# Six converted weight quarters in place of four, and landed weights as three half slabs in place of two slabs, in a two-layer hybrid decoder trunk

## The reference

```python
def even_mixer(xn, ...):                     # layer 0: w_in 1024 x 8192, w_out 2048 x 1024
    aq, af, ai, bq, bk, bv, z = split(xn @ w_in)
    oa = head_rms_norm(hgrn2_chunked(aq, af, ai, lb))     # A: gated linear recurrence, 8 heads of 128
    ob = moba_attention(rotary(bq), rotary(bk), bv)       # B: causal softmax attention, 8 heads
    return (concat(oa, ob) * silu(z)) @ w_out
def odd_mixer(xn, ...):                      # layer 1: w_in 1024 x 6144, w_out 2048 x 1024
    cx, dq, dk, dv, z = split(xn @ w_in)
    oc = rglru_branch(cx, ...)                            # C: conv of width 4, gates, scan
    od = head_group_norm(retention_chunked(dq, dk, dv))   # D: retention, 8 heads
    return (concat(oc, od) * silu(z)) @ w_out
def memory_cross_attention(xn, mem, ...):    # wq 1024 x 512, wkv 1024 x 1024, wo 512 x 1024
    return softmax(q @ k.T / sqrt(128)) @ v @ wo
```

## Time and profile before

| what | value |
|---|---|
| median of 3 runs | 611.93 us |
| profiled execution | 613.36 us, span 611.6 us |
| mean granted TensorE clock | 0.993 |
| TensorE matmul, busy | 582.0 us (95%) |
| TensorE weight load, busy | 532.1 us (87%) |
| DVE, busy | 412.6 us (67%) |
| ACT, busy | 379.4 us (62%) |
| GpSimd, busy | 44.0 us (7%) |
| weights and other loads | 97.22 MB, 46.6% of the 16 DMA engines' time |
| low parts on DVE (line 936) | 176, 1266 ns each |
| high parts on ACT (line 436) | 176, 1057 ns each |
| chain that ended last | TensorE 63%, DVE 16%, ACT 9% |

### The profile page before, as it was taken

One profiled execution on the slowest core, in us unless ns is written; L12 is line 12 of the kernel. 1 busy time (PEld: TensorE's weight loads), 2 busy tenths in 40 slices (PEclk: granted clock), 3 DMA queues, 4 the chain that ended last, 5 costly groups with the idle time before them and its releaser, 6 DMA issues.

```text
span 611.6 us, 9584 instructions
## 1 busy us (share of the span) xinstructions
PE 582.0 (95%) x3850; PEld 532.1 (87%) x3850; DVE 412.6 (67%) x618; ACT 379.4 (62%) x561; POOL 44.0 (7%) x43
## 2 busy tenths in 40 slices
PE   3999998999999999999999999999989999999984
PEld 3998997999899898889988999999879998888973
DVE  3987368636966795566657773879956962776554
ACT  5864485247257765555766747679747828565752
POOL 4001003001001000100000001105010100100000
PEclk9999999999999999999999999999989999999998
DMA  7746453445444473465335455245333553356101
GB/s 228 268 141 212 140 192 124 157 138 207 139 138 143 140 268 139 140 228 183 138 138 198 147 191 192 95 141 210 138 137 138 201 213 138 122 188 240 35 1 69
DMA packets 51871, 97.82 MB, mean 160 GB/s; under 512 B 1236, under 2 KB 7668, under 8 KB 51828
## 3 DMA queue, kind: packets, MB, share of 16 engines
q1 hardware_dynamic: 51828, 97.22, 46.6%
HBM read 96.16 MB, written 1.05 MB: 159 GB/s over the span
## 4 chain that ended last, share of the span: by engine, by line
PE 63%; DVE 16%; ACT 9%; DVEq 6%; issue 3%; ACTq 2%; DMA 1%; SPq 0%
PE proj L1527 10%; PE proj L1528 10%; PE proj L1529 10%; PE proj L1545 8%; PE proj L1547 8%; PE proj L1546 8%; DVE w_lo L936 5%; PE head L1635 4%; ACT w_hi L436 3%; PE head L1724 1%; ACT xT_hi L458 1%; DVE junk L1403 1%; DVEq L1126 1%; DVE work L1125 1%; DVE xT_lo L960 1%
## 5 line engine op out<-in xcount | busy, mean ns | idle before, releaser
L936 DVE TENSOR_TENSOR w_lo<-raw_weights,w_hi 128x1024 fp32r<-128x1024 f32 x176 | 220.5, 1266 | 140.1 <-ACT w_hi L436 138.0
L436 ACT ACTIVATE w_hi<-raw_weights 128x1024 fp32r<-128x1024 f32 x176 | 184.2, 1057 | 129.4 <-PE proj L1529 74.1
L1527 PE MATMUL proj<-xT_hi,w_hi 128*128 128x256 f32 x768 | 222.0, 289 | 2.3 <-DVE xT_lo L960 1.7
L1528 PE MATMUL proj<-xT_lo,w_hi 128*128 128x256 f32 x768 | 217.2, 283 | 0.0
L1529 PE MATMUL proj<-xT_hi,w_lo 128*128 128x256 f32 x768 | 217.2, 283 | 0.0
L1527 PEld LDWEIGHTS proj<-xT_hi,w_hi 128*128 128x128 f32 x768 | 147.1, 192 | 4.6 <-issue 3.6
L1528 PEld LDWEIGHTS proj<-xT_lo,w_hi 128*128 128x128 f32 x768 | 147.2, 192 | 0.9 <-issue 0.7
L1529 PEld LDWEIGHTS proj<-xT_hi,w_lo 128*128 128x128 f32 x768 | 147.1, 192 | 0.0
L1545 PE MATMUL proj<-w_hi,y_hi 128*128 128x512 f32 x192 | 76.2, 397 | 0.0
L1547 PE MATMUL proj<-w_lo,y_hi 128*128 128x512 f32 x192 | 74.8, 390 | 0.0
L1546 PE MATMUL proj<-w_hi,y_lo 128*128 128x512 f32 x192 | 74.8, 389 | 0.0
(11 more groups left out here) (233 smaller groups left out, 687.8 us busy)
## 6 DMA issues: line engine op xcount, KB each, us to landing
raw_weights<-in_ev_w_in_dram SPq DMA_DIRECT2D x15, 2048.0 KB, 8.5
raw_weights<-in_od_w_in_dram SPq DMA_DIRECT2D x12, 2048.0 KB, 8.0
raw_weights<-in_ev_w_out_dram SPq DMA_DIRECT2D x4, 2048.0 KB, 8.0
raw_weights<-in_xa_wkv_dram SPq DMA_DIRECT2D x4, 2048.0 KB, 8.2
raw_weights<-in_od_w_out_dram SPq DMA_DIRECT2D x4, 2048.0 KB, 7.7
raw_weights<-in_xa_wq_dram SPq DMA_DIRECT2D x2, 2048.0 KB, 9.3
raw_weights<-in_xa_wo_dram SPq DMA_DIRECT2D x2, 2048.0 KB, 8.1
raw_weights<-in_ev_w_in_dram SPq DMA_DIRECT2D x4, 512.0 KB, 5.8
```

The lines of the kernel that those rows point to most:

```text
L436: act.activation(ring_quarter(w_hi, n, q), raw_quarter(n, q), ACT.Copy).then_inc(hi_ready, 1)
L936: dve.tensor_tensor(ring_quarter(w_lo, n, q), raw_quarter(n, q), ring_quarter(w_hi, n, q).bitcast(F32), ALU.subtract).then_inc(lo_ready, 1)
L1527: pe.matmul(dst, wh[:, k, :], x_hi[:, k, :], start=(k == 0), stop=False)
L1528: pe.matmul(dst, wh[:, k, :], x_lo[:, k, :], start=False, stop=False)
```

## The change

The rings hold six quarters (`RING`), quarter m in place m mod 6. The lead of a conversion over its position grows from three quarters to five: `due(p)` gives the quarters converted at position p: p + 3 up to p = 4, then two quarters at p = 5 (8, 9), one at 6 (10), two at 7 (11, 12), and p + 5 from 8 on. The landed weights are 1 MB halves of slabs ("units", u = 2n or 2n + 1) in three places (`UNITS`) with a semaphore each; SP issues unit u when unit u - 3 is converted. The wait for slab n in SP's program (line 320) stays. The constants and positions still go out at the start of the loop's pass n = 2, so behind unit 3 and its wait. `seen_f` and `prm_rows`, used at the start, are laid over `dmask`, first written in stage D.

```diff
+RING = 6
+UNITS = 3
+
+
+def due(p):
+
+    if p < 5:
+        return [p + 3]
+    return {5: [8, 9], 6: [10], 7: [11, 12]}.get(p, [p + 5])
...
-        raw = sb("raw_weights", [P, 2, 4096])
-        w_hi = sb("w_hi", [P, 4, 1024], F32R)
-        w_lo = sb("w_lo", [P, 4, 1024], F32R)
+        raw = sb("raw_weights", [P, UNITS, 2048])
+        w_hi = sb("w_hi", [P, RING, 1024], F32R)
+        w_lo = sb("w_lo", [P, RING, 1024], F32R)
...
+        seen_f = dmask[:, 0, :]
+        prm_rows = dmask[:, 1, 0:2 * P].rearrange("p (t c) -> p t c", t=2)
...
+        def dram_unit(u):
+            n, h = divmod(u, 2)
+            w = dram_slab(n)
+            if SLABS[n][2] == "F":
+                return w[:, :, 2 * P * h:2 * P * h + 2 * P]
+            if SLABS[n][2] == "T":
+                return w[:, 4 * h:4 * h + 4, :]
+            return w[:, :, 512 * h:512 * h + 512]
+
+        def unit_landings(u):
+
+            return 16 * (u // UNITS + (u % UNITS == 2))
...
-                sp.dma_start(raw[:, n % 2, :].rearrange("p (k c) -> p k c", k=4 if SLABS[n][2] == "W" else KC),
-                             dram_slab(n)).then_inc(w_landed[n % 2], 16)
+                for u in (2 * n, 2 * n + 1):
+                    if u >= UNITS:
+                        sp.wait_ge(lo_ready, 2 * (u - UNITS) + 2)
+                    sp.dma_start(raw_unit(u, SLABS[n][2]), dram_unit(u)).then_inc(w_landed[u % UNITS], 16)
...
-            def ahead(n, q):
-
-                n, q = divmod(4 * n + q + 3, 4)
+            def high_part(m):
+
+                n, q = divmod(m, 4)
                 if n >= NSLAB:
                     return
                 if n == 0:
                     act.wait_ge(first_landed[q], 16)
-                elif q == 0:
-
-                    act.wait_ge(w_landed[n % 2], 16 * ((n + 1) // 2))
-                if n >= 1:
-                    act.wait_ge(quarter_used, 4 * (n - 1) + q + 1)
+                elif q % 2 == 0:
+
+                    act.wait_ge(w_landed[(2 * n + q // 2) % UNITS], unit_landings(2 * n + q // 2))
+                if m >= RING:
+                    act.wait_ge(quarter_used, m - RING + 1)
                 act.activation(ring_quarter(w_hi, n, q), raw_quarter(n, q), ACT.Copy).then_inc(hi_ready, 1)
+
+            def ahead(n, q):
+
+                for m in due(4 * n + q):
+                    high_part(m)
```

More of the change, by code:

```diff
@@ L104, in hybrid_trunk @@
         shared = sb("shared_rows", [P, 2048])
-        prm_rows = sb("prm_rows", [P, 2, P])
         prm = sb("prm", [P, N_ROWS])
@@ L111, in hybrid_trunk @@
         causal = sb("causal", [P, 3 * P])
-        seen_f = sb("seen_f", [P, 3 * P])
         seen = sb("seen", [P, 3 * P], I32)
@@ L140, in hybrid_trunk @@
         first_landed = [sem(f"first_landed{q}") for q in range(4)]
-        w_landed = [sem(f"w_landed{i}") for i in range(2)]
+        w_landed = [sem(f"w_landed{i}") for i in range(UNITS)]
         hi_ready = sem("hi_ready")
@@ L254, in dram_slab, with raw_unit @@
             return I["xa_wo"][layer].rearrange("(k p) n -> p k n", p=P)
+        def raw_unit(u, kind):
+            return raw[:, u % UNITS, :].rearrange("p (k c) -> p k c", k=KC if kind == "F" else 4)
+        def dram_unit(u):
[8 more added lines that the diff above has]
+            return 16 * (u // UNITS + (u % UNITS == 2))
         def raw_quarter(n, q):
             kind = SLABS[n][2]
-            r = raw[:, n % 2, :]
+            r = raw_unit(2 * n + q // 2, kind)
             if kind == "F":
[L260 to L264, removed]
+                return r[:, :, P * (q % 2):P * (q % 2) + P]
+            return r[:, 2 * (q % 2):2 * (q % 2) + 2, :]
         def ring_quarter(ring, n, q):
-            return ring[:, q, :].rearrange("p (k c) -> p k c", k=KC if SLABS[n][2] == "F" else 2)
+            return ring[:, (4 * n + q) % RING, :].rearrange("p (k c) -> p k c", k=KC if SLABS[n][2] == "F" else 2)
         def bank(n, u, half=0):
@@ L929, in _, with low_part, ahead @@
         def _(dve):
-            def ahead(n, q):
-                n, q = divmod(4 * n + q + 3, 4)
+            def low_part(m):
+                n, q = divmod(m, 4)
                 if n >= NSLAB:
                     return
-                dve.wait_ge(hi_ready, 4 * n + q + 1)
+                dve.wait_ge(hi_ready, m + 1)
                 dve.tensor_tensor(ring_quarter(w_lo, n, q), raw_quarter(n, q),
                                   ring_quarter(w_hi, n, q).bitcast(F32), ALU.subtract).then_inc(lo_ready, 1)
+            def ahead(n, q):
+                for m in due(4 * n + q):
+                    low_part(m)
             def rstd(i):
```

## The result

The changed kernel took 620.05 us in the median of 7 runs (615.81 to 620.37), the kernel before, on the same chip, 613.43 us (611.83 to 615.14). The ratio of the means is 1.0094, with a 95% interval of 1.0072 to 1.0115: slower by 0.9%, 5.7 us. I had forecast slower, 616.2 us, 4.3 more than the median of three runs, in a range up to 618.1. The direction came true, the time lies outside the range.

A forecast was written before the change was run, and what follows sets the result against it. TensorE was taken as the bound, with DVE and ACT without slack in the first 50 us. Conversions 2.3, positions 0.3 and clock 1.7 summed to 4.3 us on the median of 611.93: 616.2 us, range 611.9 to 618.1.

The forecast's parts named there:

- what a longer lead can do: Conversions wait for the same quarter with either ring; at most 1.6 us of TensorE's weight waits could be removed.
- Two more conversions ahead of the scan: DVE, before line 1611: the lead made up at positions 5 and 7 delays the scan 2.3 us, bounds 1.2 to 2.6.
- The positions: SP's queue at the start: positions land behind unit 3 and delay DVE's angles by 0.3 us, bounds 0 to 1.2.
- The fit: DMA estimate, 2 us plus bytes at 436 GB/s: 1 MB lands in 4.4 us; the trace's 4.9 was preferred.
- the weight waits of slab_t: TensorE's 1.0 us of weight waits go, but later waits for DVE grow by the saving: counted nothing, bound 1.0 gained.
- the end: Last cross-attention: two conversions vanish, DVE's and ACT's waits for TensorE grow; counted nothing, bound 1.1 us gained.
- the term of the clock: Behind stage A's first wait, grown to about 3.8 us, TensorE's clock falls to half: 1.7 us, bounds 0 and 2.4.
- the base: The sum of 4.3 us was put on the median 611.93 us, not on the profiled execution's 613.36.
- the transfer rival: Rows of 1 KB and two waits per slab make halves late, 25 slabs losing 0.3 us: 623 us; chance 0.06.
- The clock holds: Rival: the same lag at the start, but no clock fall behind the stall: 614.5 us; chance 0.20.
- No change: Rival: conversions fit DVE's hole ahead of 46.58, or weight and end gains offset them: 612.4 us; chance 0.12.
- Faster: Rival: the longer lead frees DVE and ACT in stage D, removing the 2.6 us stall: 609.2 us; chance 0.12.

The follow-up runs named there:

- e2: A with constants and positions issued ahead of unit 3's wait and the two extra conversions moved to positions 14 and 15: 613.20 us, ratio 1.000 to B.
- e3: B with DVE computing the low parts of quarters 8 and 10 twice, into an unused tile, ahead of the scan: 616.77 us, ratio 1.0059 to B.
- e9: e5 with constants and positions issued ahead of unit 3's wait and 14 fillers in the first place: 613.85 us, ratio 1.0007 to B.
- A: The changed kernel: rings of six, lead of five, half slabs, constants behind unit 3's wait; 620.05 us, ratio 1.0094 to B.
- B: The kernel before the change, with rings of four and a lead of three: 613.43 us beside A.
- e7: Half slabs in three places alone, with rings of four, lead of three and constants first: 612.61 us, ratio 0.9987 to B.
- e6: A with constants first, the longer lead taken up behind stage A's products, and filler matmuls in stage D and at the end: 611.64 us, ratio 0.9960 to B.
- e1: A with constants and positions issued ahead of unit 3's wait again: 621.11 us, ratio 1.0095 to B.
- e5: A with filler matmuls in all three stalls (15 in stage A, 12 in stage D, 2, 3 and 2 at the end): 614.22 us, ratio 1.0005 to B.
- e8: B with filler matmuls in stage D (9) and at the end (2, 3 and 2), none in stage A: 612.11 us, ratio 0.9966 to B.
- e4: A with 15 filler matmuls of ident by ident in TensorE's first stall, before line 1647: 617.26 us, ratio 1.0060 to B.

## Why the prediction was right and wrong

**Right: what a longer lead can do.** A deeper ring moves no release condition, since p + 5 with six places waits for the same quarter as p + 3 with four. e2 has the time of before to 0.2%.

**Right: where the loss starts.** Two more conversions ahead of the scan, 2.3 us; e3 shows 2.34 at the same instruction. The positions, 0.3 us with bounds of 0 and 1.2: the trace has them 0.38 later against the rest of the start, e9 gives 0.37. The wait of 3.8 us and the scan at 42.5 (42.64) came as worked out. The fit that I quoted from the Trainium skill ("DMA: Bandwidth & Descriptors", Anatomy of one DMA) is stated there for transfers issued from GpSimd, and these go out from SP. The halves landed in 5.0 to 5.5 us, 0.6 to 1.1 above its 4.4.

**Right: the weight waits of slab_t come back.** Line 1719's first wait is 1.6 us where 0.34 had been, and line 1671's 3.36 where 2.58 had been. They grew by more than the 1.0 us that was saved. The prediction was at odds with itself here: it let the wait before line 1635 grow in one place and named it "unchanged" among its signs. On the time there was little direct effect: from stage A's second wait to stage D's A takes 0.23 us more than B. That the longer wait makes the longer fall is not shown, since e7 had the long one behind 2.58 us.

**Small, as forecast: the end.** The waits of DVE and ACT that were to grow did (0.68 to 2.04 us, 0.19 to 2.55, the latter with the third fall in it). TensorE's own waits stayed, and the gain there is the 0.3 us seen in e6.

**Wrong: the term of the clock.** This is the step that failed. I had written "Price 1.7 us; bounds 0 and 2.4", for one fall behind the first stall. In A's profile that fall cost 1.54 us, inside the bounds; in e1's, behind a shorter wait, 2.83, outside them. But the sum counted only this fall. It had the wait before line 1635 and the gaps at the end as they are in B, and so put any change of the clock there at nothing, without a reason. The gaps at the end did stay; the clock in them did not, and in stage D the clock stayed down twice as long. By medians the clock cost 4.5 us more than before: the loss of 6.6 less the 2.1 of e5 against e8. The profiles say the same, 6.1 against 1.55. Where I had 1.7, the term measured 4.5, and its bounds should have taken in all three places.

**Wrong: the base.** The sum went on 611.93, the median of three runs. Two of these (611.83, 611.93) lie on the step without a fall, the third (613.43) on that with one. The median of B in later comparisons was 613.5 to 613.7. A part of the miss, 1.5 us, is that a number with steps of 1.5 us was taken as a steady one; the profiled execution, 613.36, was nearer. The fastest run of A, 615.81, is 4.0 over the fastest of B, which is near the 4.3 of the sum: lag, positions and one fall, which by its clock every run of A has.

**Wrong, and small:** the gain of rings, halves and lead was counted as nothing and is 0.5 to 0.7 us. The miss of 3.85 us is then 1.5 of base, 2.8 of clock and 0.25 of lag and positions, less 0.7. The 623 us of the transfer rival is a slip: 616.2 and 25 times 0.3 make 623.7.

**The rivals.** *The clock holds*: falls by after's trace; e5 shows what it would have been, 614.2 (I had 614.5). *No change*: the hole ahead of 46.58 took nothing. *Faster*: falls by line 1671's wait, which grew. *Transfers*: falls by e2 and e7.

That the direction came true owes little to luck: the lag of 2.3 us was worked out and found.

What stays open: why the clock fell at the end in the profiles of A, e1, e2 and e7 and not in those of B, e3 and e4, with the same waits in the same order; and why lag and lead together bring more of it than each alone. All these kernels' runs scatter in steps, so the moment at which a stall comes may count; that was not tried by itself. What the fillers show is that idle time at these places is needed for the falls.

## What to carry to other kernels

Before making a buffer deeper, compare the release condition at each position: if it names the same event as before, the producers are as tied as they were, and the extra lead must be paid once, at a place where the producer has slack (e2: taken up at positions 14 and 15 in place of 5 and 7, it cost nothing). A wait on the path of a nearly full TensorE had two prices here, its length and the clock after it. The second was paid per fall, and differed from run to run at the same stall, so it wants a range for every long stall of the kernel, also for those that the change leaves alone. When times of one kernel lie in steps, compare runs of equal mean clock, or hold the clock by filling the idle time with matmuls of no use: here that made 0.4 us visible that 5 us of scatter had hidden.

## What the runs showed of the hardware

- Times of one kernel lie in steps of about 1.5 us, and its mean granted clock with them (B: 611.9, 613.6, 615.0 and 616.4 at 0.996, 0.994, 0.991 and 0.988). The fall of the clock to half in stage A cost 1.54 us (A against e4). With fillers in the stalls the 12 runs of e8 lie within 0.33 us.
- The clock fell behind three waits of 0.49, 0.95 and 0.53 us with short transposes between them in the profiles of A, e1, e2 and e7, and did not in those of B, e3 and e4 with the same waits.
- The same stall can cost no step, one or two. Behind 2.58 us of waiting in stage D the clock held (e3), stood at half for 3.4 us (B) or for 6.8 us (e7). Behind 3.32 to 3.36 us it fell for one step in e2 and e4 (16 matmuls in 4.30 and 4.38 us) and for two in A and e1 (5.49 us); at full clock they took 2.88.
- A 1 MB half landed in 5.0 to 5.5 us, a 2 MB slab in 7.7 to 9.3 (medians by weight matrix), and the DMA engines' busy share rose only from 46.6 to 48.8% though the packets went from 51828 to 79140.
